# Two decoder blocks, expert stage: 512-wide products, expert outputs in two banks, scatters by halves of 64 rows, another order of the waves

## What is computed

```python
logits = x @ router_w + router_b
top_v, top_i = lax.top_k(logits, 2)
gate = sum(one_hot(top_i, 8) * softmax(top_v)[..., None], -2)
for e in range(8):
    out = out + gate[..., e:e + 1] * ((silu(x @ w1[e]) * (x @ w3[e])) @ w2[e])
```

## Time and profile before

| what | value |
|---|---|
| median of 3 runs | 2323.59 us (2322.94 to 2324.44) |
| the profiled execution | 2319.97 us |
| its span, first to last instruction | 2318.7 us |
| mean granted clock of TensorE | 0.976 |
| PE busy | 2205.3 us (95%) |
| DVE, ACT busy | 695.9 us, 427.9 us |
| the expert stage | about 747 to 1513 us of the span |

### The profile page before, as it was taken

The page is one execution under the profiler, slowest core; times in us unless marked ns, Lnnn a source line. Parts: engine busy times, 40 slices in busy tenths (PEclk is TensorE's granted clock), DMA queues, the critical chain, the costliest instruction groups (busy, mean ns, idle before and its releaser), DMA issues.

```text
span 2318.7 us, 36881 instructions
## 1 busy us (share of the span) xinstructions
PE 2205.3 (95%) x16193; PEld 1445.0 (62%) x16193; DVE 695.9 (30%) x1453; ACT 427.9 (18%) x972; POOL 0.2 (0%) x4
## 2 busy tenths in 40 slices
PE   8988999999878999999999999989999999989998
PEld 5664777666755766555455464555667776657775
DVE  2563366223663100110100100035526642730001
ACT  2463000113462000000000100132310002230001
POOL 0000000000000000000000000000000000000000
PEclk9988999999979999999999999989999999999999
DMA  5222987023303999899999887533179641238300
GB/s 217 103 83 102 414 326 286 0 99 134 130 1 143 424 402 388 344 395 407 371 403 419 367 342 312 203 103 116 66 303 397 253 172 55 100 128 334 139 34 19
DMA packets 55175, 523.90 MB, mean 226 GB/s; under 512 B 6368, under 2 KB 6880, under 8 KB 16864
## 3 DMA queue, kind: packets, MB, share of 16 engines
q1 hardware_dynamic: 45792, 471.13, 50.5%
q10 hardware_dynamic: 9216, 50.34, 5.8%
HBM read 520.39 MB, written 1.05 MB: 225 GB/s over the span
## 4 chain that ended last, share of the span: by engine, by line
PE 87%; DVE 7%; ACT 4%; issue 1%; DMA 1%; DVEq 0%; SPq 0%; ACTq 0%
PE ps L89 87%; DVE ring L89 5%; ACT ring L89 2%; DVE stat L89 1%; DVE natural L89 1%; ACT transposed L89 1%; DVE residual L89 0%; ACT L89 0%; DMA ring<-in_moe 0%; DVE transposed L89 0%; ACT z L89 0%; ACT natural L89 0%; ACT stat L89 0%; DMA constants<-in_const 0%; DVE gates L89 0%
## 5 line engine op out<-in xcount | busy, mean ns | idle before, releaser
L89 PE MATMUL ps<-ring 128*32 128x256 f32 (+9 forms) x7764 | 546.4, 338 | 13.6 <-ACT ring L89 3.7
L89 PEld LDWEIGHTS ps<-ring 128*32 128x32 f32 (+4 forms) x7764 | 370.3, 123 | 185.0 <-issue 66.8
L89 PE MATMUL ps<-ring,transposed 128*128 128x384 f32 (+4 forms) x1408 | 473.1, 493 | 4.0 <-ACT transposed L89 4.0
L89 PE MATMUL ps<-ring,z 128*32 128x512 f32 (+3 forms) x2048 | 474.5, 584 | 0.3 <-ACT z L89 0.3
L89 PE MATMUL ps<-transposed,ring 128*128 128x256 f32 x2112 | 466.4, 379 | 5.4 <-ACT transposed L89 4.3
L89 PEld LDWEIGHTS ps<-transposed,ring 128*128 128x128 f32 x2112 | 401.0, 190 | 85.9 <-issue 28.7
L89 PEld LDWEIGHTS ps<-ring,transposed 128*128 128x128 f32 x1408 | 262.7, 192 | 190.7 <-issue 63.7
L89 DVE TENSOR_TENSOR z<-z,ps 128x256 f32<-128x256 f32 (+3 forms) x146 | 58.8, 403 | 889.0 <-ACT z L89 859.2
L89 PEld LDWEIGHTS ps<-ring,z 128*32 128x32 f32 (+2 forms) x2048 | 175.2, 140 | 220.2 <-issue 209.7
L89 ACT ACTIVATE z<-ps 128x256 f32<-128x256 f32 (+2 forms) x151 | 56.4, 373 | 942.9 <-PE ps L89 923.0
L89 ACT COPY z<-ps 128x384 f32<-128x384 f32 (+6 forms) x166 | 68.0, 410 | 653.4 <-PE ps L89 651.8
(11 more groups left out here) (123 smaller groups left out, 923.2 us busy)
## 6 DMA issues: line engine op xcount, KB each, us to landing
ring<-in_moe SPq DMA_DIRECT2D x88, 2048.0 KB, 12.0
ring<-in_ffn SPq DMA_DIRECT2D x66, 1536.0 KB, 13.8
ring<-in_moe SPq DMA_DIRECT2D x88, 1024.0 KB, 10.8
ring<-in_w_in SPq DMA_DIRECT2D x26, 1536.0 KB, 6.3
z<-in_ada ACTq DMA_DIRECT2D x48, 768.0 KB, 6.1
ring<-in_w_out SPq DMA_DIRECT2D x12, 1536.0 KB, 7.0
natural<-in_ada ACTq DMA_DIRECT2D x16, 768.0 KB, 8.1
ring<-in_ple_gate SPq DMA_DIRECT2D x4, 1536.0 KB, 6.5
```

The lines of the kernel that those rows point to most:

```text
L89: self.ins = None if self.book.counting else op(*args, **kw)
```

## The change

Four things are changed in the expert stage. The two halves of a wave become k 0 to 3 and k 4 to 7, and each product streams w1 and w3 together, from two places 2048 elements apart, up to 512 wide (`piece_ups`). For 96 tokens an expert has nine waves: eight of four jobs of two blocks, and a last one of two jobs of one block, so that there are 65 waves. The output of such an expert lies in two banks: tokens 0 to 63 in one, with the halves of the features over each other, and tokens 64 to 95 in the other, with even and odd blocks apart; the scatter's product over 64 rows adds the two. A gather and a gates are one task, and a scatter two (one for each `i`), over banks 7 and 4; its two halves of the features come from rows 0 to 63 and 64 to 127. And the waves of experts 5 to 7 are spread over experts 0 to 3: six with expert 0, then four with each of the others; expert 4 runs alone.

```diff
+    def piece_ups(n, k, block, blocks):
+
+        at = 2 * P * k + (block % 2) * P
+        return piece(n)[:, 0:4 * D].rearrange("p (h n) -> p h n", h=2)[:, :, at:at + blocks * P]
+
...
-        jobs = [[(t, 2 * p, 2) for p in range(4 * s, 4 * s + 4) for t in range(3)] for s in range(2)]
-        jobs.append([(t, b, 1) for b in range(16, FB) for t in range(3)])
-        return [[(32 * g, 32, 32 * t, b, n) for g, (t, b, n) in enumerate(part[w:w + 4])] for part in jobs for w in range(0, len(part), 4)]
+        pairs = [(t, 2 * p, 2) for p in range(NPIECE) for t in range(3)][0:-1]
+        jobs = [pairs[w:w + 4] for w in range(0, len(pairs), 4)] + [[(2, FB - 2, 1), (2, FB - 1, 1)]]
+        return [[(32 * g, 32, 32 * t, b, n) for g, (t, b, n) in enumerate(wave)] for wave in jobs]
...
-        for x, y in zip(*LANES):
-            for a, b in ((2, 1),) * 6 if CAP[x] == P else ((3, 2), (3, 2), (5, 2)):
-                yield from waves[x][:a]
-                yield from waves[y][:b]
-                waves[x], waves[y] = waves[x][a:], waves[y][b:]
-            yield from waves[x] + waves[y]
-        for x in LANES[0][len(LANES[1]):]:
-            yield from waves[x]
+        between = [wave for y in LANES[1] for wave in waves[y]]
+        for x in LANES[0]:
+            size = 2 if CAP[x] == P else 3
+            for w in range(0, len(waves[x]), size):
+                n = 2 if CAP[x] == 96 and w == 0 else 1
+                yield from waves[x][w:w + size]
+                yield from between[0:n]
+                between = between[n:]
+        assert not between
...
-            waiting += [(2 * FIRST_WAVE[x] - 1, 2 * start, ("gather", x, half), None) for half in range(2)]
+            waiting.append((2 * FIRST_WAVE[x] - 1, 2 * start, ("gather", x, 0), None))
...
-            waiting += [(2 * LAST_WAVE[x] + 2, 2 * FIRST_WAVE[x] + 2, ("gates", x, i), None if b is None else ("scatter", b, 3))
-                        for i in range(NT)]
+            waiting.append((2 * LAST_WAVE[x] + 2, 2 * FIRST_WAVE[x] + 2, ("gates", x, 0), None if b is None else ("scatter", b, 1)))
             if x != LANES[0][-1]:
-                waiting += [(2 * LAST_WAVE[x] + 16, 2 * LAST_WAVE[x] + 5, ("scatter", x, n), ("gates", x, 1)) for n in range(4)]
+                waiting += [(2 * LAST_WAVE[x] + 16, 2 * LAST_WAVE[x] + 5, ("scatter", x, i), ("gates", x, 0)) for i in range(NT)]
...
-    AUX = aux_order()
+    AUX, AUX_BANKS = aux_order(), (7, 4)
...
-    mo_pickg, mo_pick = mw(NT, 3, P), mw(NT, P)
-    mo_gT, mo_y = (mw(NT, 3, P), mw(NT, 1, P)), (mw(3, 512), mw(1, 512))
+    mo_pickg, mo_pick = mw(NT, 2, P), mw(NT, P)
+    mo_gT, mo_y = (mw(NT, 2, P), mw(NT, 1, P)), (mw(2, 512), mw(1, 512))
...
+    def gather_banks(x):
+        return (6, 7) if x == 0 else AUX_BANKS
...
-        for k in range(4):
-            for i in range(NT):
-                at = (4 * half + k) * P
-                mm(ps[:, 6 + half if x == 0 else 7, k * CAP[x]:(k + 1) * CAP[x]], xn[:, i, at:at + P], mo_pick[:, i, 0:CAP[x]],
-                   i == 0, i == NT - 1)
-        pe.then_inc(f"mo.gather{x}{half}")
-
-    def dve_mo_xg(x, half):
+        for half in range(2):
+            for k in range(4):
+                for i in range(NT):
+                    at = (4 * half + k) * P
+                    mm(ps[:, gather_banks(x)[half], k * CAP[x]:(k + 1) * CAP[x]], xn[:, i, at:at + P], mo_pick[:, i, 0:CAP[x]],
+                       i == 0, i == NT - 1)
+            pe.then_inc(f"mo.gather{x}{half}")
...
-            out, places = row_places(x, i)
-            dve(V.tensor_scalar, out, places, ro_pos[:, x, i:i + 1], ro_gate[:, x, i:i + 1], ALU.is_equal, ALU.mult)
+            for out, places in ((mo_pickg[:, i, 0, :], C("slots")),) if CAP[x] == P else (
+                    (mo_pickg[:, i, 0, :].rearrange("p (a t) -> p a t", a=2), spread(C("slots")[:, 0:64], 1, 2)),
+                    (mo_pickg[:, i, 1, :].rearrange("p (a t) -> p a t", a=4), spread(C("slots")[:, 64:96], 1, 4)))[0:CAP[x] // 32 - 1]:
+                dve(V.tensor_scalar, out, places, ro_pos[:, x, i:i + 1], ro_gate[:, x, i:i + 1], ALU.is_equal, ALU.mult)
...
+    def out_banks(x):
+        return 2 if CAP[x] > 64 else 1
+
+    def gate_blocks(x):
+        return 2 if CAP[x] == 96 else 1
...
-        for b in range(3 if CAP[x] == 96 else 1):
-            turn(7, b * P, mo_pickg[:, i, b, :])
-        pe.then_inc(f"mo.gates{x}{i}")
+        for i in range(NT):
+            for b in range(gate_blocks(x)):
+                turn(AUX_BANKS[i], b * P, mo_pickg[:, i, b, :])
+        pe.then_inc(f"mo.gates{x}")
...
+            act.wait_ge(f"mo.scatter{before(x)}1")
+        for i in range(NT):
+            act(S.copy, mo_gT[lane(x)][:, i, 0:n, :], ps[:, AUX_BANKS[i], 0:n * P].rearrange("p (b t) -> p b t", b=n))
+        act.then_inc(f"mo.gates.done{x}0")
...
-        if CAP[x] == P:
-            rows = [(q, 0, P)]
-        elif CAP[x] == 96:
-            rows = [(0, 0, P), (1, 0, 64)] if q == 0 else [(1, 64, P), (2, 0, P)]
-        else:
-            rows = [(0, 64 * q, 64 * q + 64)]
-        for m, (b, lo, hi) in enumerate(rows):
-            mm(ps[:, bank_, :], mo_gT[lane(x)][lo:hi, i, 0 if CAP[x] == P else b, :], mo_y[lane(x)][lo:hi, b, :],
-               m == 0, m == len(rows) - 1)
-        pe.then_inc(f"mo.scatter{x}{n}")
+        blocks = gate_blocks(x)
+        for b in range(blocks):
+            for q in range(2):
+                lo, hi, at = (0, P, q) if CAP[x] == P else (64 * q, 64 * q + 64, b)
+                mm(ps[:, banks[q], :], mo_gT[lane(x)][lo:hi, i, b, :], mo_y[lane(x)][lo:hi, at, :], b == 0, b == blocks - 1)
+        pe.then_inc(f"mo.scatter{x}{i}")
...
-        dve.wait_ge(f"mo.scatter{x}{n}")
-        dve_add_residual(n // 2, n % 2, ps[:, bank_, :]).then_inc(f"mo.scatter.done{x}{n}")
+        dve.wait_ge(f"mo.scatter{x}{i}")
+        for q in range(2):
+            dve_add_residual(i, q, ps[:, AUX_BANKS[q], :])
+        dve.then_inc(f"mo.scatter.done{x}{i}")
...
-        for half in range(2):
-            for k in range(KD):
-                for row, width, token, block, n in jobs:
-                    mm(ps[row:row + width, g % 2, half * 2 * P:half * 2 * P + n * P], expert_tokens(x, k)[:, token:token + width],
-                       piece_up(PIECES.index((x, block // 2)), half, k, block, n), k == 0, k == KD - 1)
-            if half == 0:
+        for k in range(KD):
+            for row, width, token, block, n in jobs:
+                mm(ps[row:row + width, g % 2, :].rearrange("p (h n) -> p h n", h=2)[:, :, 0:n * P], expert_tokens(x, k)[:, token:token + width],
+                   piece_ups(PIECES.index((x, block // 2)), k, block, n), k == 0, k == KD - 1)
+            if k == KD // 2 - 1:
...
         if CAP[x] == 96:
-            for a in range(12):
-                block, row = 2 * p + (a // 3) % 2, 32 * (a % 4)
-                mm(ps[row:row + 32, 2 + a // 4, :], turned_block(x, 32 * (a % 3), block), piece_down(n, block, a // 6),
-                   p == 0, p == NPIECE - 1)
+            for b in range(2):
+                for q in range(2):
+                    for t in range(2):
+                        row = 64 * q + 32 * t
+                        mm(ps[row:row + 32, 2, :], turned_block(x, 32 * t, 2 * p + b), piece_down(n, b, q),
+                           p == b == 0, p == NPIECE - 1 and b == 1)
+            for q in range(2):
+                for b in range(2):
+                    row = 64 * q + 32 * b
+                    mm(ps[row:row + 32, 3, :], turned_block(x, 64, 2 * p + b), piece_down(n, b, q), p == 0, p == NPIECE - 1)
...
-            act.wait_ge(f"mo.scatter{before(x)}3")
-        for b in range({P: 2, 96: 3, 64: 1}[CAP[x]]):
+            act.wait_ge(f"mo.scatter{before(x)}1")
+        for b in range(out_banks(x)):
...
-    LAST_BANKS = (0, 1, 6, 7)
+    LAST_BANKS = ((0, 1), (6, 7))
...
-        for n in range(4):
-            dve.wait_ge(f"mo.scatter{LAST}{n}")
-            dve_add_residual(n // 2, n % 2, ps[:, LAST_BANKS[n], :]).then_inc(f"ple1.h{n // 2}{n % 2}")
+        for i in range(NT):
+            dve.wait_ge(f"mo.scatter{LAST}{i}")
+            for q in range(2):
+                dve_add_residual(i, q, ps[:, LAST_BANKS[i][q], :]).then_inc(f"ple1.h{i}{q}")
```

More of the change, by code:

```diff
@@ L1602, in pe_route @@
         pe_ple_product(1)
-        for half in range(2):
-            pe_mo_gather(0, half)
+        pe_mo_gather(0)
     def dve_beats(out, x, n):
@@ L1647, in dve_order @@
         dve(V.tensor_copy, most_i, ro_sm[:, 0:1]).then_inc("route.most")
-        for half in range(2):
-            dve_mo_xg(0, half)
+        dve_mo_xg(0)
         dve.part("route")
@@ L1698, in dve_mo_select, with pe_mo_gather, dve_mo_xg @@
         dve.then_inc(f"mo.pick{x}")
-    def pe_mo_gather(x, half):
+    def gather_banks(x):
+        return (6, 7) if x == 0 else AUX_BANKS
+    def pe_mo_gather(x):
         pe.part("mo")
         pe.wait_ge(f"mo.pick{x}")
-        if x == 0 and half == 0:
```

(40 more changed lines are left out.)

31 lines of the change are left out of this document (19 added, 12 removed).

## The result

| | before | after |
|---|---|---|
| median | 2324.02 us (2322.94 to 2325.28, 4 runs) | 2287.14 us (2286.8 to 2287.6, 4 runs) |
| ratio, 95% interval | | 0.9841 [0.9824, 0.9858] |
| the profiled execution | 2319.97 us | 2287.38 us |
| its span | 2318.7 us | 2286.0 us |
| up to PE's first product of the expert stage | 747.06 us | 745.79 us |

The changed kernel is faster by 1.6%, 36.9 us in the medians. The forecast was 2286.6. The stage is shorter by 37.55 us, forecast 37.0. Between the two profiled executions there are 32.6 us, not the 37.0 of the forecast, since the rest is 6.2 longer; that is taken up at the end.

The account below looks back on a forecast made before the run. PE's work in the expert stage was taken as the bound. Terms 20.3 + 4.6 + 1.8 + 2.1 + 5.3 + 1.0 + 2.4 - 0.5 = 37.0 us off 2319.97 give 2283.0, plus 3.6 for the median: 2286.6; range 2281 to 2298.

Parts of the forecast that it names:

- Scatters (20.3): Expert stage on PE: 64-row products run side by side, 1.05 us for 64 tokens, 1.91 for 96; 20.3 us saved.
- side tasks: Gates and gathers on PE: 16 gates tasks become 8, 14 gathers 7, eight fewer transposes; 2.4 us saved, up to 3.9.
- the pairs don't overlap: Rival on the scatters: 64-row pairs do not overlap at 512 columns; 18.9 us come back, 2305.5 us; chance 0.06.
- End of the stage (4.6): Last copies, scatters and transpose: 0.6, 4.0 and 0.69 us saved, one add of 0.69 exposed; sum 4.6.
- Waves and turns (1.8 and 2.1): 96-token waves repacked over four experts: 1.8 us saved, and eight fewer transposes save 2.1.
- Issue stalls (5.3): PE's issue waits in narrow waves, put to instruction rate under full DMA: 5.3 us saved, bounds 3.3 and 5.8.
- 512 wide (1.0): Products streaming 512 instead of 256 columns: 1 us saved, between 0 and 2.5.
- restarting stream: Rival: split w1/w3 operand costs each of 928 wide steps an entry of 0.1 us, 93 us, 2380; chance 0.03.
- wide steps over 0.45: Sign in the changed profile: 512-column steps taking over 0.45 us would make the forecast wrong.
- The rule on weight loads: Rival by the skill's rule: weight loads lie in the open, 3,960 fewer save some 200 us more, 2087; chance 0.01.
- Weights (0.5 against): Experts 1 to 3: 55 pieces need 410 us of DMA, PE 431; PE stays bound, short bunches cost 0.5 us.
- All after it unchanged: Expected sign in the changed profile: the stage shorter by 37 us and everything behind it unchanged.

Follow-up runs that it names:

- scatters-only kernel: Kernel before with only two-bank outputs, scatters by 64-row halves and joined side tasks; waves, order and 256-wide products kept: 2302.71 us, ratio 0.9921.
- packing alone: Kernel before with only the new jobs of the 96-token waves, nine waves instead of eleven, still 256 wide, old lane order: 2315.08 us, ratio 0.9968.
- old order: Changed kernel with the old order of the lanes, experts 3 and 4 alone: 2293.34 us, ratio 0.9877.
- packing undone: Changed kernel with the old 96-token waves, six of two blocks and five of one, w1 and w3 still streamed together: 2290.81 us, ratio 0.9869.
- scatters-only stage with 20 more: Kernel before with only the scatter, output and side-task changes, plus 20 short DVE instructions in the never-taken branch: 2298.87 us, ratio 0.9913; stage 743.08 us.
- other scatter loop: Changed kernel with the scatter's two loops exchanged, both blocks of one feature half first: 2285.37 us, ratio 0.9845.
- never-run code: Changed kernel with 14 or 26 short DVE instructions added to the never-taken branch: 2294.19 us (ratio 0.9894) and 2285.86 us (ratio 0.9856).

## Why the prediction was right

- **The bound.** PE stayed the bound, as argued; the chain is 87% PE, and the 60 us of the dense stretch are full.
- **How near, and how much of it is luck.** The mechanism held term by term, but the closeness is in part luck. The stage's 37.55 for 37.0 has 1.5 more from the widening, and 1.6 of both numbers are the clock's at the last scatters, which the forecast took for the length of the products. The forecast for an execution like the profiled one was 2283.0, and it took 2287.38; the median of 2287.14 for 2286.6 is as close as it is because two misses met: the changed kernel's profiled execution came out 4.4 us longer than forecast, the rest above all, and the 3.6 us added for the median did not come.
- **Scatters (20.3).** Measured 1.92 for 1.91 at 96 tokens; at 64 tokens 1.06 for 1.05; expert 0's 1.86 for 1.91. Shown: the scatters-only kernel without DVE's second stall has a stage 26.4 us shorter, against 26.6 for scatters, end of stage and side tasks together without the 0.7 of the last transpose. (That 0.7 is the packing's, not the order's, as the prediction has it: the wait is gone with the packing alone and with the old order, and back, 0.68, with the packing undone. The side tasks' 2.4 have no measurement of their own.) The rival that the pairs don't overlap is out, and the kernel before had it on show at 512 columns: its last scatters wrote four banks, and there two products of 64 rows, four instructions, took 1.1 us (by shape, window 1510.18 to 1511.20):

```profile
L89 PE MATMUL ps<-z 64*128 64x512 f32 x4 | 1.1, 641 | 0.0
```

- **End of the stage (4.6).** The scatters 4.12 shorter for 4.0, the copies 0.62 for 0.6, the transpose's wait gone, and the add in the open cost 0.85 for 0.7. But the 7.82 us that the forecast started from had 3.4 us at 1.2 GHz in them. At the full clock the old scatters take 6.21 (packing alone), so 2.5 of the 4.1 are the change's and 1.6 the clock's.
- **Waves and turns (1.8 and 2.1).** The last wave of two jobs takes 1.83 us (1457.73 to 1459.56) and at most 1.76 (to 1461.68, with two instructions of w2 among its own): 3.6 for 3.66. The wide halves are as priced.
- **Issue stalls (5.3).** Shown by the packing alone (no issue wait; 9.3 of stage without the clock's 1.6, for 9.9 from waves, turns, stalls and the last transpose) and by the packing undone under wide products (no issue wait either, with the DMA engines full). So the rate of instructions is needed, but it isn't enough: the kernel before has the same narrow waves in experts 3 and 4, and there no issue wait, at a DMA share of 0.96 and 0.45 (1468 to 1492) instead of 1.01 (the scatters-only kernel has one, 0.56 us, in expert 3, at 0.98):

```profile
1365.00:1391.00 26.00, 25.90 (x613) 17.87 (x609) 1.15 (x4) 2.28 (x8) 0.00 (x0) 1.00 0.96 389
```

  All five stalls of the kernel before lie in experts 1 and 2, where both come together, as the prediction had it. The trace has 40 packets for PE in the stage, where it had 68:

```profile
q8 instruction: 40, 0.66, 0.4%
```

- **512 wide (1.0).** This is the term that was mis-sized: 2.5 us. I had 0 to 2.5 from the earlier trace rows and took a value below the middle, where the whole difference a step was real. The rival of the restarting stream is out: a wide step has 232.7/512 = 0.4545 us busy, less than the 0.457 that it was priced at. The prediction's own sign of being wrong, "wide steps over 0.45", was set wrongly: it lies below that price, and the measured step is over it although the forecast held.
- **The rule on weight loads.** The Trainium skill, TensorE: Matmul & The Clock Gate, What overlaps and what doesn't, has weight loads overlap a product only in other row groups; then 3,960 fewer of them would have given some 200 us. The gain was 37, and halving them for the up products alone gave 2.5. The trace disagrees with the rule here.
- **Weights (0.5 against).** No wait for weights inside the stage behind the first piece, a share of 0.92 in the dense stretch, and 7.5 us of stage lost with the old order: 5.2 in waits and 3.1 by the clock behind them, less 0.8 that no row names. That the spread order keeps the room is shown.
- **The parts don't quite add.** 26.4 (the scatters-only stage with 20 more), 10.9 and 2.5 make 39.8, and the stage has 37.55. Joined with the new order, scatters and packing gave 35.0 (769.46 less 734.48) where alone they gave 37.3. Of the 2.3, the 1.6 of the clock at the last scatters are counted in both parts. What is left, 0.7, is hardly more than the two profiles of the kernel before differ by (769.46 and 770.05).
- **"All after it unchanged" was wrong.** The rest took 808.3 and 808.6 us in two profiles of the changed kernel, 802.1 and 802.3 in two of the kernel before. In that stretch PE had the lower clock (1.2 GHz) for 44 us against 31, and 13 us more at half speed cost some 6.5, about what the rest is longer by. It isn't the faster stage: the same with 256-wide products has 802.7, with the other scatter loop 802.4, with never-run code 803.9 and 804.2. Whether it hangs on the code or on the execution stays open. For the code speak the pairs of profiles. For the execution speaks the run with the old order: its profile, an execution of 2300.13 us, has a rest of 808.5 and again 44 us of the lower clock, while the same kernel's other three executions took 2292.5 to 2293.5. The kernel before, too, took from 2316.8 us (clock 0.978) to 2326.9 (0.973) in 13 executions on one chip. The medians don't show the 6 us as a loss: the profiled execution of before lay 4 us under its median, that of after at its median, so that the 37.55 + 1.27 - 6.19 = 32.6 us between the profiled executions stand beside 36.9 in the medians.

## What to carry to other kernels

Where one engine's stream is the bound, price each edit from start to start in its timeline and then hold the new pace against the transfers: here, once the products were faster, the order of the waves was worth 7 us, and the wider product 2.5. A wait of 2 to 3 us on the bound engine can cost half as much again, or more, by the clock behind it. Products on disjoint halves of the rows that write different banks run side by side, so lay the operands of two products of 64 rows each on the two halves. When two versions differ by 5 us, look for a single issue stall behind a jump before you explain it by the edit: a branch that is never taken can move it.

## What the runs showed of the hardware

- **The fetch of instructions shows in the time.** Behind the jump DVE waits 2.2 to 2.5 us in every kernel, and 4.7 to 5.8 more where it lands 2 to 7 instructions ahead of one place in its code (by inference the end of a page); where it lands 18 or 20 ahead, or behind that place, there was none. Under full DMA (share 1.01), PE stood up to 1.55 us in narrow waves; at 0.96 and 0.45 the same waves in the kernel before had no such wait. The Trainium skill, Runtime: NRT & Kernel Launch, Instruction fetch mechanics, calls the fetch hidden, but says in the same section that a taken branch whose target isn't in the fetched window stalls for it. The first wait behind the jump agrees with that; the stall some instructions later is one that these runs add to it.
- **PE runs the two halves of the rows side by side also where the queue has the products of one half next to each other**: 1.92 us for eight instructions in both orders. With the other loop the second half's first instruction is the fifth in the queue; how much farther ahead that reaches wasn't tried.
- **A short wait of PE can cost the clock too.** With the old order, two waits of 2.19 and 3.05 us for weights were each followed by 3.4 us at a granted clock of 0.5 (1.2 GHz), 1.7 and 1.4 us more. A wait of 1.94 us ahead of the last scatters was followed by it in two profiles of the kernel before and not with the packing alone.
